# Two-layer branch decoder on one core: a reordered opening, squares summed on VectorE, and forty modulation tiles multiplied in pairs of high and low parts

## The chip, the cores and the metric

The kernel runs on one core of one Trainium2 chip. The metric is the device time of one execution in microseconds; the figure for a kernel is the median of its runs.

## What is computed

Two layers act on 520 token vectors of 1024 channels (512 prompt positions, 8 sample positions). There are nine conditioning vectors: one for the prompt, one for each sample. Cut to what matters:

```python
def trunk_layer(x, c, ...):
    mod = (jax.nn.silu(c) @ ada_w + ada_b)[:, None, :]            # 1024 -> 6 * 1024
    shift1, scale1, gate1, shift2, scale2, gate2 = jnp.split(mod, 6, axis=-1)
    h = rmsnorm(x, norm_g[0]) * (1.0 + scale1) + shift1
    z = h @ w_in
    ...                                 # three branches with gates, merged
    x = x + gate1 * (merged @ w_out)
    h2 = rmsnorm(x, norm_g[1]) * (1.0 + scale2) + shift2
    x = x + gate2 * peer(h2, peer_w_query, peer_sub_keys, peer_u, peer_v)
```

`rmsnorm` needs, for each token, the sum over 1024 channels of x². A final `rmsnorm` follows the second layer. All arithmetic is float32.

## The kernel before

**Layout.** A matrix is cut into tiles of 128 output channels by 1024 inputs (512 KB); channels lie on partitions in KC = 8 chunks of 128. A float32 tile is split into a high part, rounded to fp32r by ScalarE (`split` of `act`, L612, or `split_m`, L886), and a low part, the rest, by VectorE (`split` of `dve`, L993). TensorE multiplies high by high, high by low and low by high in `both` (L1515, L1516, L1518). One *product* is a tile times all tokens: 8 chunks, two halves of 260 tokens, 48 matmuls. Weights stand in a ring of four slots (`raw`, `w_hi`, `w_lo`); SyncE loads a tile once the one four before is split.

**Order.** Each engine's program is written out by hand, and semaphores join them. A layer's products are steps: `T_V` (0 to 3, gMLP v, done as tokens by channels in `v_parts`, L1610 to L1612), `T_U` (4), `T_B` (8), `T_C` (16), `T_BB` (24 to 27), `T_BR` (28 to 63: three branches b of 12 steps), `T_O` (64 to 71), then the query steps, 128 blocks up and 128 blocks down (L1827 to L1829).

**Modulation.** `ada_w` of a layer is 48 tiles. They are multiplied in plain float32, with the 9 columns of `cond_silu` stationary and the tile streaming. The first 16 (shift1 and scale1 of layer 1) go in four batches of four in `first_ada` (L1551). The other 80 are slipped in one by one behind products (`ada_tile`, L1567), by a table that gives each tile a step: `OWN_STEPS` for this layer's, `NEXT_STEPS` for the next layer's. Tiles come over ScalarE's DMA queue into the two slots of `ada_raw` (`load_ada`, L654). A batch of four tiles leaves a 9 x 512 row; ScalarE copies it out (`ada_rows`, L646), TensorE turns it by four transposes (`ada_turn`, L1576) and VectorE adds the bias (`take_ada`, L1047).

**Norms.** ScalarE squares a chunk of x (`square`, L631) into one of two buffers; TensorE sums over partitions with a stationary matrix of ones (`square_sum`, L1542), two float32 matmuls for each chunk; ScalarE takes the root (`std`, L637), VectorE inverts it (`root`, L1010), and `norm` and `modulate` form the new high and low parts (L1020, L679, L1025). There are five norms: two in each layer, and the final one, of which only the sums matter here. In this text norm 1 is layer 1's first, norm 2 its second, and so on to norm 5.

**Opening.** SyncE loads the conditions, the first batch, the biases (`ada_par`), the second batch, x, and batches three and four. GpSimd loads `par` and the convolution histories at once, ScalarE the first two `ada_raw` tiles. TensorE does batch, turn, batch, turn, four sums, batch, turn, four sums, batch, turn, and waits for `norm`.

**End of a layer.** The last down block releases the eight chunks of x one after another (L1494); ScalarE first splits one more tile, then loads the root's table and squares.

In the steps `T_BB` and `T_BR` VectorE also works off the 31-tap convolution, one instruction for each tap (L1179, `conv_c`), by the tables `BB_TAPS` and `BR_TAPS`.

## Time and profile before

| | us |
|---|---|
| runs (3): median, lowest, highest | 4106.55, 4103.54, 4110.15 |
| the profiled execution: its time | 4103.9 |
| its span, first to last instruction | 4102.1 |
| TensorE matmul busy | 4008.8 (98%) |
| VectorE busy | 2732.5 (67%) |
| ScalarE busy | 1584.2 (39%) |
| GpSimd busy | 812.4 (20%) |
| mean granted TensorE clock | 0.995 |

The profile is one execution recorded by the hardware. A row of a timeline gives start and duration in us, engine, line, operation, output and input tiles, a count of merged instructions and, in brackets, how long the engine had been idle and what ended that. Matmul durations overlap, since matmuls are pipelined: the spacing of starts is what one costs. A float32 matmul stands in the records twice, an fp32r matmul once.

### The profile page before, as it was taken

Reading aid. Unit: us, or ns where it says so; the run is one execution under the profiler, and the core shown is the slowest. Engines: PE = TensorE matmul, PEld = TensorE weight load, DVE = VectorE, ACT = ScalarE, POOL = GpSimd, SP = SyncE. Lnnn points to the kernel's source line nnn. Section 1 sums busy time; section 2 is a strip of 40 time slices with the busy share of each in tenths; the row PEclk is TensorE's granted clock in tenths of the full one; section 3 lists DMA queues with packets and bytes.
Section 4 is the critical chain, followed back from the end, with each engine's and each line's share of the span. In section 5 each row is a group of like instructions: output and inputs, shape, how many; then the busy total and the mean of one; then the engine's idle time right before and its main releaser. Section 6 shows DMA issues by size and latency. Waiting matters only on the chain.

```text
span 4102.1 us, 77256 instructions
## 1 busy us (share of the span) xinstructions
PE 4008.8 (98%) x29632; PEld 3893.8 (95%) x29632; DVE 2732.5 (67%) x4453; ACT 1584.2 (39%) x2673; POOL 812.4 (20%) x685
## 2 busy tenths in 40 slices
PE   6999999999999999999999999999999999999998
PEld 3899999999999999999989999899999999999998
DVE  2367638977666636777753775698776664477776
ACT  2222323333577733333332223333337775333332
POOL 1000000000122206555300000000002221356551
PEclk9999999999999999999999999999999999999999
DMA  4444332354466668999934532225445667799995
GB/s 171 140 113 134 103 117 77 118 166 136 128 190 193 192 202 315 345 352 352 336 128 114 134 109 83 78 89 170 136 137 160 187 190 208 238 352 345 352 349 185
DMA packets 418219, 781.87 MB, mean 191 GB/s; under 512 B 151184, under 2 KB 274448, under 8 KB 417344
## 3 DMA queue, kind: packets, MB, share of 16 engines
q1 hardware_dynamic: 176640, 441.70, 33.4%
q10 hardware_dynamic: 194240, 196.10, 15.2%
q0 software_dynamic: 47104, 141.00, 9.5%
q8 instruction: 140, 2.29, 0.3%
q14 instruction: 95, 0.78, 0.1%
HBM read 655.79 MB, written 122.88 MB: 190 GB/s over the span
## 4 chain that ended last, share of the span: by engine, by line
PE 95%; DVE 3%; ACT 1%; DMA 1%; issue 1%; DVEq 0%; SPq 0%; ACTq 0%; POOLq 0%
PE pg L1515 20%; PE pg L1518 19%; PE pg L1516 19%; PE pm L1827 5%; PE pg L1829 4%; PE pg L1828 4%; PE pm L1829 4%; PE pm L1828 4%; PE pg L1827 4%; PE pm L1567 3%; PE pm L1779 2%; DVE ys L1179 1%; PE pm L1542 1%; PE pm L1743 1%; DMA merged<-stream 1%; PE pm L1551 1%
## 5 line engine op out<-in xcount | busy, mean ns | idle before, releaser
L1515 PE MATMUL pg<-a_hi,w_hi 128*128 128x260 f32 x6400 | 1684.6, 284 | 25.1 <-DVE a_lo L1025 14.4
L1516 PE MATMUL pg<-a_lo,w_hi 128*128 128x260 f32 x6400 | 1667.2, 282 | 0.0
L993 DVE TENSOR_TENSOR w_lo<-raw,w_hi 128x1024 fp32r<-128x1024 f32 x688 | 841.2, 1225 | 1003.8 <-ACT w_hi L886 703.0
L1518 PE MATMUL pg<-a_hi,w_lo 128*128 128x260 f32 x6400 | 1290.0, 283 | 0.5 <-issue 0.5
L1515 PEld LDWEIGHTS pg<-a_hi,w_hi 128*128 128x128 f32 x6400 | 1208.7, 189 | 41.1 <-issue 37.1
L1516 PEld LDWEIGHTS pg<-a_lo,w_hi 128*128 128x128 f32 x6400 | 1205.6, 188 | 0.3
L1518 PEld LDWEIGHTS pg<-a_hi,w_lo 128*128 128x128 f32 x6400 | 987.1, 189 | 0.3 <-issue 0.2
L886 ACT CAST w_hi<-raw 128x1024 fp32r<-128x1024 f32 x500 | 525.7, 1051 | 784.9 <-PE pg L1829 739.6
L570 POOL DMA_INDIRECT rows<-stream,at_v x256 | 282.1, 1102 | 766.0 <-DVE acc_tok L1442 317.7
L580 POOL TENSOR_TENSOR one_j<-one_j,g_lo 128x896 fp32r<-128x896 f32 x112 | 189.3, 1690 | 1034.9 <-ACTq L914 1034.9
L618 ACT ACTIVATE hid<-pg 128x260 f32<-128x260 f32 x512 | 170.7, 386 | 517.0 <-PE pg L1518 497.1
L574 POOL DMA_INDIRECT hid_pick<-hid_tok,at_e x256 | 302.5, 1182 | 255.1 <-DMA hid_tok<-hid 177.7
L1442 DVE SCALAR_TENSOR_TENSOR acc_tok<-rows,coef,acc_tok 128x1024 f32<-128x1024 f32 x254 | 327.1, 1288 | 26.9 <-DVE hid_in L1425 12.0
L612 ACT CAST w_hi<-raw 128x1024 fp32r<-128x1024 f32 x188 | 196.2, 1048 | 323.8 <-PE pg L1518 298.4
L911 ACT ACTIVATE one_j<-one_j,g_hi 128x128 fp32r<-128x128 f32 x784 | 242.1, 390 | 163.1 <-DVEq L1409 163.1
L1179 DVE SCALAR_TENSOR_TENSOR ys<-glu,par,ys 128x512 f32<-128x512 f32 x240 | 180.3, 751 | 8.8
L1827 PE MATMUL pm<-h_hi,w_hi 128*128 128x392 f32 x512 | 177.4, 347 | 2.1 <-issue 2.1
L1827 PE MATMUL pm<-a_hi,w_hi 128*128 128x392 f32 x512 | 178.1, 348 | 0.0
L1829 PE MATMUL pg<-h_hi,w_lo 128*128 128x392 f32 x512 | 175.0, 342 | 0.0
L1829 PE MATMUL pm<-h_hi,w_lo 128*128 128x392 f32 x512 | 174.8, 341 | 0.0
L1827 PE MATMUL pg<-a_hi,w_hi 128*128 128x392 f32 x512 | 174.8, 341 | 0.0
L1828 PE MATMUL pg<-h_lo,w_hi 128*128 128x392 f32 x512 | 174.7, 341 | 0.0
(234 smaller groups left out, 5598.3 us busy)
## 6 DMA issues: line engine op xcount, KB each, us to landing
raw<-stream SPq DMA_DIRECT2D x688, 512.0 KB, 4.1
hidden_dram<-hid SPq DMA_DIRECT2D x256, 196.0 KB, 3.5
gate_dram<-gate_buf ACTq DMA_DIRECT2D x28, 1792.0 KB, 11.0
hid_in<-hidden_dram ACTq DMA_DIRECT2D x64, 784.0 KB, 6.1
gate_in<-gate_dram ACTq DMA_DIRECT2D x64, 784.0 KB, 11.0
ada_raw<-stream ACTq DMA_DIRECT2D x76, 512.0 KB, 3.4
hid_tok<-hid SPq DMA_DIRECT2D x256, 64.0 KB, 3.6
rows<-stream,at_v POOLq DMA_INDIRECT x256, 7.3
```

Source lines behind the costliest of these rows:

```text
L570: pool.indirect_dma_start(rows[:, k % ROWS, :], None, rows_v, bass.IndirectOffsetOnAxis(ap=at_v[:, k:k + 1], axis=0)).then_inc(row_in[k % ...
L574: pool.indirect_dma_start(hid_pick[:, k:k + 1], None, hid_elems, bass.IndirectOffsetOnAxis(ap=at_e[:, k:k + 1], axis=0)).then_inc(elem_in[ ...
L886: act.copy(ring(True, m % 4), raw[:, m % 4]).then_inc(hi_ready, 1)
L911: own.do(act.activation(one_j[:, n % 2, 0, t, :], one_j[:, n % 2, 1, t, :].bitcast(F32), ACT.Copy, scale=g_hi[:, n * GS + t:n * GS + t + 1 ...
L993: tt(ring(False, s), raw[:, s], ring(True, s).bitcast(F32), ALU.subtract).then_inc(lo_ready, 1)
L1442: dve.scalar_tensor_tensor(out=acc_tok[:, :], in0=v, scalar=coef[:, k:k + 1], in1=acc_tok[:, :], op0=ALU.mult, op1=ALU.add).then_inc(row_u ...
L1515: pe.matmul(outs[h], w[0], a[h][0], start=first, stop=False)
L1516: pe.matmul(outs[h], w[0], a[h][1], start=False, stop=False)
L1518: mm = pe.matmul(outs[h], w[1], a[h][0], start=False, stop=last)
L1827: pe.matmul(out, w_hi[:, j, d, :], hi[:, j, :], start=first, stop=False)
L1828: pe.matmul(out, w_hi[:, j, d, :], lo[:, j, :], start=False, stop=False)
L1829: mm = pe.matmul(out, w_lo[:, j, d, :], hi[:, j, :], start=False, stop=last)
```

## The change

1. **Opening.** The batches go in the order 2, 3, 0, 1 (scale first). x is loaded second; GpSimd's loads wait for the last batch, ScalarE's `ada_raw` loads come after `std`. TensorE does one batch, the eight sums, then the other three back to back with the turns in their middles, each batch in a PSUM bank of its own. The last turn moves behind chunk 0 of `v_parts`. `norm` scales chunks before the shifts are there.
2. **Pairs.** Forty of the 80 tiles are multiplied two at a time. ScalarE makes their high parts (`pair_hi`), VectorE the low ones (`pair_lo`), in buffers that overlay `merged` (early) or `ys` (late). The stationary operand is `c_parts`: 9 high and 9 low columns of the conditions. A pair is 16 fp32r matmuls of 256 columns (`ada_pair`). The row is then 18 x 512, and the turn is four float32 matmuls with `both_parts` (two stacked identities), which also add high and low rows. Pairs stand at steps 3, 5, 7, 9, 11, 13, 25, 27 (layer 2: from 7) and, for the next layer, at 53, 55, 57, 59, 61, 63. The 40 other tiles stay single.
3. **Sums of squares.** VectorE adds squares of chunks (`add_square`), so that TensorE sums fewer: 2 in place of 8 in norms 2 and 4, 6 in place of 8 in norms 3 and 5. Squares no longer wait for TensorE (their buffers reach into `merged`).
4. **Layer end.** ScalarE's last `split` goes behind the squares.
5. In layer 1 the two loads for step 5 are issued between ScalarE's splits of step 4's tiles.

```diff
-OWN_STEPS = (3, 3, 4, 5, *range(6, 14), *range(T_BB, T_BR), *range(T_BR, T_BR + 16))
+FIRST_ORDER = (2, 3, 0, 1)
+PAIR_EARLY, PAIR_LATE = (3, 5, 7, 9, 11, 13, T_BB + 1, T_BB + 3), tuple(range(T_BR + 25, T_O, 2))
+OWN_STEPS = (*(w for w in PAIR_EARLY for _ in range(2)), *range(T_BR, T_BR + 16))
 GAP_1, GAP_2 = T_V + 1, T_O + KC
-NEXT_STEPS = (*range(T_BR + 24, T_O + 2), GAP_2, GAP_2)
+NEXT_STEPS = (*(w for w in PAIR_LATE for _ in range(2)), T_O, T_O + 1, GAP_2, GAP_2)
...
+def sq_groups(j):
+    if j == 0:
+        return [[n] for n in range(KC)]
+    return [[*range(KC - 1)], [KC - 1]] if j % 2 else [[0], [1], [2], [3, 4], [5, 6], [7]]
...
-        ada_row = sb(ctx, "ada_row", [NC, 512])
+        ada_row = sb(ctx, "ada_row", [2 * NC, 512])
+        both_parts = sb(ctx, "both_parts", [2 * NC, NC])
+        c_parts = sb(ctx, "c_parts", [P, KC, 2 * NC], F32R)
...
+        early_hi = sb(early_pair, "early_hi", [P, 2, KC, P], F32R)
+        early_lo = sb(early_pair, "early_lo", [P, 2, KC, P], F32R)
...
+            if b < FIRST_BATCHES:
+                return pg[:, b // 2, b % 2]
...
-            for b in range(FIRST_BATCHES):
-                sp.dma_start(first_tiles[b], stream[4 * b:4 * b + 4].rearrange("n p k m -> p n k m")).then_inc(first_in[b], 16)
+            for b, n in enumerate(FIRST_ORDER):
+                sp.dma_start(first_tiles[b], stream[4 * n:4 * n + 4].rearrange("n p k m -> p n k m")).then_inc(first_in[b], 16)
                 if b == 0:
+                    sp.dma_start(x[:, :, :], x_t).then_inc(x_in, 16)
                     sp.dma_start(ada_par[:, :, :], ada_params).then_inc(ada_par_in, 16)
-                if b == 1:
-                    sp.dma_start(x[:, :, :], x_t).then_inc(x_in, 16)
...
+            own.link(pool.tensor_tensor(both_parts[:, :], ident[0:2 * NC, 0:NC], ident[0:2 * NC, NC:2 * NC], ALU.add))
...
+                    pool.wait_ge(first_in[FIRST_BATCHES - 1], 16)
...
-                if n >= 2:
-                    act.wait_ge(sq_used, l * (2 * KC) + (base * KC + n - 1))
+                if l + base == 0 and n >= 2:
+                    act.wait_ge(sq_used, n - 1)
...
-                act.activation(sq[:, n % 2, :], x[:, k, :], ACT.Square).then_inc(sq_ready, 1)
+                act.activation(square_of(l * 2 + base, n), x[:, k, :], ACT.Square).then_inc(sq_ready, 1)
...
+            def pair_hi(l, w):
+                g = pair_at(l, w)
+                if g is None:
+                    return
+                act.wait_ge(ada_used, g)
+                if w == PAIR_EARLY[0] or (l and w == PAIR_EARLY[2]):
+                    act.wait_ge(a_part, l * (2 * KC) + KC)
+                if w == PAIR_LATE[0]:
+                    act.wait_ge(y_ready, l * 3 + 2)
+                for z in range(2):
+                    n = RAW_TILES.index(g + z)
+                    act.wait_ge(ada_in[n % 2], (n // 2 + 1) * 16)
+                    act.copy(pair_parts(w)[0][:, z], ada_raw[:, n % 2]).then_inc(pair_hi_ready, 1)
...
+                if l == 0 and w == 0:
+                    act.wait_ge(mod_taken, FIRST_BATCHES)
+                    for k in range(4):
+                        prompt(k, k + 1)
+                    ada_rows(3)
+                    act.wait_ge(mod_taken, FIRST_BATCHES + 1)
+                    for k in range(4, KC):
+                        if k == 6:
+                            of_samples(KC + 1)
+                        prompt(k, k + 1)
+                    return
...
+                    act.wait_ge(x_in, 16)
+                    square(l, 0, 0)
+                    square(l, 0, 1)
+                    ada_rows(0)
+                    for n in range(2, KC):
+                        square(l, 0, n)
+                    std(l, 0, 1.0 / D)
                     for g in loads_first(0):
                         load_ada(g)
-                    ada_rows(0)
                     ada_rows(1)
-                    act.wait_ge(x_in, 16)
-                    for n in range(4):
-                        square(l, 0, n)
+                    for k in range(4):
+                        split(l, 0, k)
                     ada_rows(2)
-                    for n in range(4, KC):
-                        square(l, 0, n)
-                    split(l, 0, 0)
-                    split(l, 0, 1)
-                    ada_rows(3)
-                    split(l, 0, 2)
-                    split(l, 0, 3)
...
+                    act.wait_ge(prod, (l - 1) * NM + (M_ED + NBLK))
+                    split(l, 0, 3)
+                    std(l, 0, 1.0 / D)
...
+                freed = loads_at(l, T_U)
                 for k in range(4):
                     split(l, 1, k)
+                    if freed and k % 2:
+                        act.wait_ge(ada_used, before(freed[k // 2]) + 1)
+                        load_ada(freed[k // 2])
...
-                for block in range(NBLK - 4 if l == DEPTH - 1 else NBLK):
+                for block in range(NBLK - 4 if l == DEPTH - 1 else NBLK - 1):
...
+                        scaled(k)
+                        if k:
+                            split(l, k - 1, k - 1)
+                    take_ada(2)
+                    scaled(4)
+                    low(0, 1)
+                    split(l, 3, 3)
+                    for k in range(1, 4):
+                        low(k, k + 1)
+                        scaled(k + 4)
+                    scaled_samples()
+                    take_ada(3)
+                    shifted_samples()
+                    low(4, 5)
+                    low(5, 6)
+                    low_samples(7)
+                    low(6, 8)
+                    low(7, 9)
...
+            def add_square(l, base, n):
+                dve.wait_ge(sq_ready, l * (2 * KC) + (base * KC + n + 1))
+                group = next(g for g in sq_groups(l * 2 + base) if n in g)
+                sum_ = square_of(l * 2 + base, group[0])
+                own.link(tt(sum_, sum_, square_of(l * 2 + base, n), ALU.add))
+                if n == group[-1]:
+                    dve.sem_inc(sq_added, 1)
...
+            def pair_lo(l, w):
+                g = pair_at(l, w)
+                if g is None:
+                    return
+                hi, lo = pair_parts(w)
+                for z in range(2):
+                    dve.wait_ge(pair_hi_ready, 2 * pairs_before(g) + z + 1)
+                    tt(lo[:, z], ada_raw[:, RAW_TILES.index(g + z) % 2], hi[:, z].bitcast(F32), ALU.subtract).then_inc(pair_lo_ready, 1)
...
+                    take_ada(0)
+                    dve.wait_ge(x_in, 16)
+                    root(0)
+                    take_ada(1)
                     scale_of(l, 0)
-                    dve.wait_ge(x_in, 16)
-                split(l, 2, 2)
-                split(l, 3, 3)
...
+                    if k >= 2:
+                        add_square(l, 1, k - 1)
...
+                for n in (4, 6):
+                    add_square(l + 1, 0, n)
...
-                if b >= 2:
-                    pe.wait_ge(mod_taken, b)
                 for k in range(KC):
+                    if b >= 2 and k == KC // 2:
+                        ada_turn(b - 1)
...
+            def ada_pair(g):
+                b, h = g // 4, g % 4 // 2
+                if h == 0:
+                    pe.wait_ge(mod_taken, b)
+                pe.wait_ge(pair_lo_ready, 2 * pairs_before(g) + 2)
+                out = ada_bank(b)[0:2 * NC, 2 * h * P:2 * (h + 1) * P].rearrange("p (s m) -> p s m", s=2)
+                for k in range(KC):
+                    for z, part in enumerate(pair_parts(TILE_STEP[g][1])):
+                        mm = pe.matmul(out, c_parts[:, k, :], part[:, :, k, :], start=k + z == 0, stop=k + z == KC)
+                mm.then_inc(ada_used, 2)
...
+                    if paired(4 * b):
+                        mm = pe.matmul(to, ada_row[:, s * P:(s + 1) * P], both_parts[:, :], start=True, stop=True)
+                    else:
+                        mm = pe.transpose(to, ada_row[0:NC, s * P:(s + 1) * P], ident[0:NC, 0:NC])
...
+                    first_ada(0)
+                    for n in range(KC):
+                        square_sum(l, 0, n)
+                        if n == 3:
+                            ada_turn(0)
+                    first_ada(1)
+                    first_ada(2)
+                    first_ada(3)
...
+                    if l == 0 and k == 0:
+                        ada_turn(3)
...
-                    if k >= 2:
-                        square_sum(l, 1, k - 2)
-                square_sum(l, 1, KC - 2)
+                square_sum(l, 1, 0)
                 gap = tiles_at(l, GAP_2)
                 for g in gap[0:1]:
                     ada_tile(g)
-                square_sum(l, 1, KC - 1)
+                square_sum(l, 1, 1)
```

TensorE at the opening (`first_ada` L1551, turn L1576, sums L1542), before:

```order
L1551 MATMUL pm<-raw,cond_silu 9x512 x8
L1576 MATMUL pm<-ident,ada_row 128x9 x4
L1551 MATMUL pm<-merged,cond_silu 9x512 x8
L1576 MATMUL pm<-ident,ada_row 128x9 x4
L1542 MATMUL pm<-sq,ones 128x260 x8
L1551 MATMUL pm<-ys,cond_silu 9x512 x8
L1576 MATMUL pm<-ident,ada_row 128x9 x4
L1542 MATMUL pm<-sq,ones 128x260 x8
L1551 MATMUL pm<-last_first,cond_silu 9x512 x8
L1576 MATMUL pm<-ident,ada_row 128x9 x4
L1610 MATMUL pm<-w_hi,a_hi 128x512
```

The same place now (L1723, L1764, L1714; `v_parts` from L1804):

```order
L1723 MATMUL pg<-raw,cond_silu 9x512 x8
L1714 MATMUL pm<-sq,ones 128x260 x8
L1764 MATMUL pg<-ident,ada_row 128x9 x4
L1714 MATMUL pm<-sq,ones 128x260 x8
L1723 MATMUL pg<-merged,cond_silu 9x512 x8
L1723 MATMUL pg<-ys,cond_silu 9x512 x4
L1764 MATMUL pg<-ident,ada_row 128x9 x4
L1723 MATMUL pg<-ys,cond_silu 9x512 x4
L1723 MATMUL pg<-last_first,cond_silu 9x512 x4
L1764 MATMUL pg<-ident,ada_row 128x9 x4
L1723 MATMUL pg<-last_first,cond_silu 9x512 x4
L1804 MATMUL pm<-w_hi,a_hi 128x512
```

All eight sums now stand ahead of three of the four batches, and one turn has left this stretch.

VectorE in steps 26 and 27 of layer 1 (L1193: take a product; L993: low part of a weight tile; L1179: taps), before:

```order
L1193 TENSOR_TENSOR ys<-pg,ys 128x260 x2
L993 TENSOR_TENSOR w_lo<-raw,w_hi 128x1024
L1179 SCALAR_TENSOR_TENSOR ys<-glu,par,ys 128x512 x6
L1193 TENSOR_TENSOR ys<-pg,ys 128x260 x2
L993 TENSOR_TENSOR w_lo<-raw,w_hi 128x1024
L1179 SCALAR_TENSOR_TENSOR ys<-glu,par,ys 128x512 x6
```

Now (L1352, L1094 and L1338 are the same three; L1191 is `pair_lo`):

```order
L1352 TENSOR_TENSOR ys<-pg,ys 128x260 x2
L1191 TENSOR_TENSOR early_lo<-ada_raw,early_hi 128x1024 x2
L1094 TENSOR_TENSOR w_lo<-raw,w_hi 128x1024
L1338 SCALAR_TENSOR_TENSOR ys<-glu,par,ys 128x512 x6
L1352 TENSOR_TENSOR ys<-pg,ys 128x260 x2
L1094 TENSOR_TENSOR w_lo<-raw,w_hi 128x1024
L1338 SCALAR_TENSOR_TENSOR ys<-glu,par,ys 128x512 x6
```

Two low parts of modulation tiles stand ahead of the split and the taps.

## Rows read from the trace of the kernel before

**Rows 1.** Page, part 1: busy us (share of the span), instructions

```profile
PE 4008.8 (98%) x29632; PEld 3893.8 (95%) x29632; DVE 2732.5 (67%) x4453; ACT 1584.2 (39%) x2673; POOL 812.4 (20%) x685
```

**Rows 2.** Timeline of TensorE, opening: start us, us, instruction, [idle before, releaser]

```profile
16.65 8.62 PE L1551 MATMUL pm<-raw,cond_silu 128*9 128x512 f32 x16 [16.65 <-DMA raw<-stream]
26.91 7.04 PE L1551 MATMUL pm<-merged,cond_silu 128*9 128x512 f32 x16 [0.45 <-DMA merged<-stream]
35.36 3.89 PE L1542 MATMUL pm<-sq,ones 128*128 128x260 f32 x16 [0.24 <-ACT sq L631]
59.30 0.38 PE L1576 MATMUL pm<-ident,ada_row 9*128 9x9 f32 x4 [0.80 <-ACTq L647]
70.52 0.77 PE L1610 MATMUL pm<-w_hi,a_hi 128*128 128x512 f32 x1 [10.84 <-DVE a_lo L1025]
```

**Rows 3.** SyncE's issues (start us), then DMA issues of the opening (KB, us to landing)

```profile
3.30 0.43 SPq L456 DMA_DIRECT2D merged<-stream  x1
5.24 13.22 SPq L456 DMA_DIRECT2D last_first<-stream  x1
...
merged<-stream SPq DMA_DIRECT2D x1, 2048.0 KB, 23.6
last_first<-stream SPq DMA_DIRECT2D x1, 2048.0 KB, 36.9
```

**Rows 4.** Stretches: us, busy us of each engine, PEclk, DMA share, GB/s

```profile
60.00:74.00 14.00, 3.48 (x8) 2.81 (x9) 13.48 (x20) 7.40 (x12) 0.00 (x0) 0.53 0.24 76
115.00:119.00 4.00, 4.00 (x23) 3.08 (x21) 0.00 (x0) 0.00 (x0) 0.00 (x0) 0.57 0.48 166
```

**Rows 5.** Timeline of TensorE: step 4 of layer 1, and of layer 2

```profile
114.51 2.72 PE L1567 MATMUL pm<-ada_raw,cond_silu 128*9 128x128 f32 x16 [4.27 <-DMA ada_raw<-stream]
...
2137.98 0.39 PE L1515 MATMUL pg<-a_hi,w_hi 128*128 128x260 f32 x1 [3.18 <-DVE w_lo L993]
```

**Rows 6.** Timeline of ScalarE, each row once a product has ended: steps with a tile, then without

```profile
266.90 1.04 ACT L612 CAST w_hi<-raw 128x1024 fp32r<-128x1024 f32 x1 [6.73 <-PE pg L1518]
274.68 1.04 ACT L612 CAST w_hi<-raw 128x1024 fp32r<-128x1024 f32 x1 [6.74 <-PE pg L1518]
...
429.61 0.67 ACT L618 ACTIVATE sig<-pg 128x260 f32<-128x260 f32 x2 [5.29 <-PE pg L1518]
...
435.37 0.67 ACT L618 ACTIVATE sig<-pg 128x260 f32<-128x260 f32 x2 [3.86 <-PE pg L1518]
```

**Rows 7.** Timeline of TensorE: seven fp32r matmuls of 256 columns, and what follows

```profile
1342.77 1.00 PE L1779 MATMUL pm<-one_j,one_i 128*128 128x256 f32 x7
1343.60 0.28 PE L1515 MATMUL pg<-a_hi,w_hi 128*128 128x260 f32 x1
```

**Rows 8.** Page, part 5: two groups, busy us, mean ns, idle before

```profile
L993 DVE TENSOR_TENSOR w_lo<-raw,w_hi 128x1024 fp32r<-128x1024 f32 x688 | 841.2, 1225 | 1003.8 <-ACT w_hi L886 703.0
...
L1179 DVE SCALAR_TENSOR_TENSOR ys<-glu,par,ys 128x512 f32<-128x512 f32 x240 | 180.3, 751 | 8.8
```

**Rows 9.** Timelines of VectorE (two `T_O` steps) and TensorE (norm 2), layer 1

```profile
603.93 0.17 DVE L1277 TENSOR_TENSOR tmp<-pg,mod 128x8 f32<-128x8 f32 x1 [3.98 <-PE pg L1518]
...
610.56 0.17 DVE L1277 TENSOR_TENSOR tmp<-pg,mod 128x8 f32<-128x8 f32 x1 [3.98 <-PE pg L1518]
...
616.99 1.92 PE L1542 MATMUL pm<-sq,ones 128*128 128x260 f32 x8
```

**Rows 10.** Timelines of TensorE (norms 3 and 5) and VectorE (last four x chunks)

```profile
2090.09 7.60 PE L1542 MATMUL pm<-sq,ones 128*128 128x260 f32 x32 [3.16 <-ACT sq L631]
...
4082.07 7.53 PE L1542 MATMUL pm<-sq,ones 128*128 128x260 f32 x32
...
4081.42 2.71 DVE L1494 SCALAR_TENSOR_TENSOR x<-pg,mod,x 128x512 f32<-128x512 f32 x4
```

**Rows 11.** `ada_raw` loads: all 76 (least, median, most us to landing); one issued in 255 to 264 us

```profile
DMA to landing us min/median/max: 3.1/3.4/14.6
...
ada_raw<-stream ACTq DMA_DIRECT2D x1, 512.0 KB, 13.1
```

More of the change, by code:

```diff
@@ L91, in tiles_at, with paired, pair_at, pairs_before @@
     return [g for g in TILE_STEP if TILE_STEP[g] == (l, w)]
+def paired(g):
+    return TILE_STEP.get(g, (0, 0))[1] in PAIR_EARLY + PAIR_LATE
+def pair_at(l, w):
+    return next((g for g in tiles_at(l, w) if paired(g)), None)
+def pairs_before(g):
+    return sum(paired(i) for i in TILE_STEP if i < g) // 2
 def before(g):
```

131 lines of the change are left out of this document (91 added, 40 removed).

## Prediction

> **What bounds the kernel now.** I read the page's busy times first: TensorE's matmuls fill 98% of the span [rows 1]. So a step that TensorE sheds is time gained, unless another engine then makes it wait. The timeline of TensorE shows the waits: one cluster is in the opening, where matmuls begin at 16.65 and the products (`v_parts`) only at 70.52, after 10.84 us of waiting for norm 1 [rows 2]. Its clock was 0.53 from 60 to 74 us and 0.57 from 115 to 119 us, so part of both stretches ran at 1.2 GHz in place of 2.4; each follows an idle spell [rows 2, 4, 5]. Elsewhere the cost of a piece is read from the spacing of steps.
>
> **The sum, part by part.** All figures are from the profiled execution.
>
> *A. Opening.* SyncE's queue lands in order. The second batch landed at 3.30 + 23.6 = 26.9, the last at 5.24 + 36.9 = 42.1, with three 2 MB transfers (x, batch three, batch four) in between and after: 5.1 us each [rows 3]. The first came at 16.65, while GpSimd's and ScalarE's loads ran beside it [rows 2]. Those now start later, so for the first batch I take an issue at 3.3 at the latest, 5.1, and 0.8 for the ramp, 9.2 (bounds: 16.65 if nothing improves, 8.4 without a ramp), 14.3 for x, 19.6, 24.7 and 29.8 for the rest. From there TensorE is the chain, with its data always ahead: first batch 8.6, eight sums 2 x 3.89 = 7.8, three batches at 7.04 and three turns at about 0.5 with their gaps [rows 2]: 9.2 + 8.6 + 7.8 + 21.1 + 1.5 = 48.2. ScalarE's row copies, four splits, and VectorE's scaled chunks fit beside the last two batches if the four weight tiles land by about 42 (alone they would at 34.9). `v_parts` starts at about 48.3 in place of 70.5: 22.2. TensorE arrives there without an idle spell, so the slow start goes: from 70.52 it ran at half clock to 74 and a little beyond, 4 us, worth 2.0. The fourth turn now stands inside `v_parts`: -0.5. **A = 23.7.** What is late next: shift chunks 4 to 7 (`take_ada(3)`) are wanted 11 us after the start and ready in about 5.
>
> *B. Pairs.* A step with a tile takes 274.68 - 266.90 = 7.78, one without 435.37 - 429.61 = 5.76 [rows 6]: a tile costs 2.02, two 4.04. A pair is 16 fp32r matmuls of 256 columns; no row has such a pair, the nearest are seven of 256 columns in 1343.60 - 1342.77 = 0.83, or 0.119 each [rows 7]: 1.90. It could be as dear as two tiles (4.04); below 1.90 I see no reason in the rows. 20 pairs x 2.14 = 42.8. The Trainium skill (TensorE: Matmul & The Clock Gate, section Back-to-back issue gap) gives 81 ns a matmul at 128 columns and 131 ns at 512 in a stream with weight loads; interpolated that is an estimate of about 98 ns at 256 columns, a pair at 1.57 and 6.6 us more gain; rows 7 speak against it.
>
> Ten batches now turn by float32 matmuls. Four transposes took 0.38 [rows 2]; four float32 matmuls are eight records. Between no more than now and eight at a single tile's 0.12 (+0.6) I take +0.35: -3.5. At step 3 of layer 1 two tiles covered a wait for the first split of step 4: layer 2, with no tile there, waited 3.18 [rows 5]. A pair covers 1.9: -1.3.
>
> VectorE and ScalarE get 40 more passes each; VectorE's is 1.22 [rows 8]. Steps 24 to 27 are the tight place: four takes (about 0.8), four splits, 22 taps at 0.75 and four low parts make 3.2 + 4.9 + 16.5 + 4.9 = 29.5 for VectorE [rows 8], against 4 x 5.76 + 2 x 1.90 = 26.8 for TensorE (31.1 before). The backlog of 2.7 is hidden, since weights are split up to three steps ahead, and from step 28 on single tiles are back (7.78 a step against 7 taps and a split, 6.5). The pair at step 27 has another problem: its loads are issued only after the pair at 25, in a stretch where a load took 13.1 to land [rows 11]. A pair is due two products, 11.5, after its loads; the second cast (1.04 [rows 6]) after the first, and the second low part, take 3.3; so it waits once landing exceeds 8.2. At 13.1 that is 4.9; at the median 3.4 it is 0. I take 1.5 for layer 1 and none for layer 2. **B = 42.8 - 3.5 - 1.3 - 1.5 = 36.5.**
>
> *C. Step 4 of layer 1.* TensorE waited 4.27 there for a tile, and then ran at a clock of 0.57 over 4 us, that is at half for 3.4 of them, 1.7 lost [rows 4, 5]. Step 4 has no tile now, and step 5's loads are issued some us earlier. **C = 6.0**, between 4.3 and 6.0.
>
> *D. Norms 2 and 4.* The steps of `T_O` are 610.56 - 603.93 = 6.63 apart [rows 9]; less 5.76 a sum costs 0.88 (0.93 back to back [rows 9]). Six fall away in norm 2: 5.3. In norm 4 the sixth was followed by a wait for the last square anyway, so I count five: 4.4. VectorE's adds (520 columns, some 0.65 by the 1.22 of 1024 [rows 8]) lie in its idle 3.98 of each step [rows 9]. **D = 9.7.**
>
> *E. Norm 3.* TensorE idled 3.16 for the first square and summed for 7.60 [rows 10]. The idle came from ScalarE, which split a tile and loaded a table first; with the split behind, squares follow x. Two sums fewer are 1.9. **E = 5.0**; the chain to norm and products behind it moves as one. Bound below: 1.9, if squares are still late.
>
> *F. Norm 5.* No idle there [rows 10], so two of eight sums: **F = 1.9**. VectorE finishes x at 4084.1 and two adds at 4085.5; the last sum but one would be wanted at 4085.8.
>
> Sum: 23.7 + 36.5 + 6.0 + 9.7 + 5.0 + 1.9 = 82.8. Against the profiled 4103.9 that gives 4021.1. The median of the runs is 2.65 above that execution, so for a median I say 4023.8.
>
> **Rivals.**
> 1. *The opening's weights are late.* GpSimd's and ScalarE's 2.7 MB now compete with the four weight tiles. Before, the same traffic moved the second batch from about 14.3 to 26.9, 12.6 us [rows 3]. Put on the tiles' 34.9 it gives 47.5; then split 1.0, row copy and turn 1.1 and half a batch 3.5: start at 53.2, 4.9 later, 4029. For it: the same bytes. Against: fewer wide transfers are in flight. The Trainium skill (DMA: Bandwidth & Descriptors, section Issuing engines are not separate DMA queues) says that transfers of all engines end on the same 16 engines and interleave, which is this rival's way; at equal shares that page would have the tiles done near 40, in time (an estimate).
> 2. *Pairs run faster* than rows 7, by the page's spacing named above: 4023.8 - 6.6 = 4017.
> 3. *Pairs save nothing*: with 18 stationary columns, or by waits, a pair costs its 4.04. B's 36.5 goes: 4060. Against it: rows 7.
> 4. *Slower than before: modulation loads bind.* 15 of the 20 pairs have their loads issued only after the pair before them. Each us of landing above 8.2 costs TensorE 15 us. At 13.7 on average the whole gain is gone; at 14.6, the longest seen [rows 11], it is 15 x 6.4 = 96, and 4120. Against it: the median is 3.4.
>
> **How the numbers follow.** Forecast 0.79, rival 1 0.12, rival 2 0.04, rival 3 0.04, rival 4 0.01. Low end: turns free (3.5), no wait at 27 (1.5), pairs by rival 2 (6.6) and a bit of run scatter: 4010. High end: rival 1 (+4.9), waits of 4.9 at step 27 in both layers (+8.3), turns at their upper bound (+2.5), scatter of 3: 4042. Rivals 3 and 4 are left out. A measurement of this kernel tells about 0.2% (8 us) from no change. Every case but the fourth is faster by more: faster 0.98, same 0.01, slower 0.01.
>
> **What would show it.** `v_parts` starting at 47 to 53 us with the clock full; 16 pair matmuls within 1.9; a turn of a paired batch within 0.6 to 1; steps with a pair 13.4 for two; no idle at step 4; 6.6-us `T_O` steps at 5.8; sums of norm 3 starting with no gap. Wrong would be: idle of TensorE in front of pairs, named by VectorE's low parts; a lower clock in the trunk; or TensorE behind VectorE's taps after step 24.

## The result, and the profile after

The changed kernel takes 4056.58 us (median of 4 runs, 4055.82 to 4058.12) against 4106.21 for the kernel before beside it: a ratio of 0.9879, 95% interval 0.9862 to 0.9896. That is 49.6 us saved where 82.8 were forecast; the predicted 4024 us and its range of 4010 to 4042 lie below. The profiled spans are 4102.1 and 4054.6, a gain of 47.5 us. Some of the runs below stood beside slower executions of the kernel before (4124.04 and 4130.88 us), so those are judged by their ratio to it and by a gain that leaves the experts out.

The page's busy line is in [rows 1]. The same line now:

```profile
PE 3969.7 (98%) x29288; PEld 3871.9 (95%) x29288; DVE 2789.2 (69%) x4510; ACT 1621.4 (40%) x2714; POOL 818.9 (20%) x686
```

TensorE's busy time fell by 39.1 us; the rest of the gain is waiting. TensorE's timeline of the opening [rows 2], step 4 of each layer [rows 5], and the last sum of norms 2 and 4 and the first of norm 5 [rows 9, 10]:

```profile
10.41 8.75 PE L1723 MATMUL pg<-raw,cond_silu 128*9 128x512 f32 x16 [10.41 <-DMA raw<-stream]
22.91 0.41 PE L1764 MATMUL pg<-ident,ada_row 9*128 9x9 f32 x4
80.77 0.39 PE L1681 MATMUL pg<-a_hi,w_hi 128*128 128x260 f32 x1 [1.34 <-DVE w_lo L1094]
...
2089.41 0.58 PE L1681 MATMUL pg<-a_hi,w_hi 128*128 128x260 f32 x1 [3.19 <-DVE w_lo L1094]
...
575.50 1.14 PE L1714 MATMUL pm<-merged,ones 128*128 128x260 f32 x4
2568.25 1.15 PE L1714 MATMUL pm<-merged,ones 128*128 128x260 f32 x4 [1.22 <-ACT merged L688]
4036.65 1.92 PE L1714 MATMUL pm<-sq,ones 128*128 128x260 f32 x8
```

The first batch is there at 10.41 in place of 16.65, `v_parts` begins at 48.66 in place of 70.52, and the stall of 4.27 us at step 4 of layer 1 is gone. The new trouble shows in TensorE's timeline of steps 25 to 29, where [rows 6] had a steady 7.78 a step. Both layers:

```profile
225.98 0.28 PE L1752 MATMUL pm<-early_hi,c_parts 128*18 128x256 f32 x1
240.75 0.29 PE L1752 MATMUL pm<-early_hi,c_parts 128*18 128x256 f32 x1 [1.25 <-DVE early_lo L1191]
248.45 1.05 PE L1762 MATMUL pm<-both_parts,ada_row 18*128 18x9 f32 x8
256.60 3.39 PE L1739 MATMUL pm<-ada_raw,cond_silu 128*9 128x128 f32 x16 [7.09 <-DMA ada_raw<-stream]
...
2250.81 0.40 PE L1752 MATMUL pm<-early_hi,c_parts 128*18 128x256 f32 x1 [3.46 <-DVE early_lo L1191]
2266.80 3.52 PE L1739 MATMUL pm<-ada_raw,cond_silu 128*9 128x128 f32 x16 [4.69 <-DMA ada_raw<-stream]
```

The pair of step 27 waits, and the single tile of step 28 waits longer. One stretch of layer 1 and two of layer 2 (columns as in [rows 4]) give the clock there: near 0.5 over some 7 us each, the lower of its levels 1.2 and 2.4 GHz, from within the wait on; the tile of step 28 takes 3.39 and 3.52 us in place of 1.92.

```profile
253.00:260.00 7.00, 3.40 (x17) 2.12 (x17) 3.88 (x6) 1.71 (x3) 0.00 (x0) 0.52 0.59 218
...
2249.00:2256.00 7.00, 5.19 (x25) 4.21 (x26) 6.29 (x8) 2.98 (x4) 0.00 (x0) 0.55 0.20 75
2263.00:2270.00 7.00, 3.20 (x16) 2.02 (x16) 3.87 (x6) 1.71 (x3) 0.00 (x0) 0.52 0.58 211
```

What issues the late load is in ScalarE's timeline, and whom ScalarE waited for:

```profile
228.11 0.82 ACTq L714 DMA_DIRECT2D ada_raw<-stream  x2
236.40 1.05 ACT L729 CAST early_hi<-ada_raw 128x1024 fp32r<-128x1024 f32 x1 [9.16 <-DMA ada_raw<-stream]
238.39 1.05 ACT L729 CAST early_hi<-ada_raw 128x1024 fp32r<-128x1024 f32 x1 [0.94 <-DMA ada_raw<-stream]
...
253.35 0.82 ACTq L714 DMA_DIRECT2D ada_raw<-stream  x2
254.22 0.67 ACT L675 ACTIVATE sig<-pg 128x260 f32<-128x260 f32 x2 [10.83 <-DVEq L1357]
```

The two loads for the pair of step 27 leave at 228.11 and are 8 to 10 us on the way. The loads for steps 28 and 29 could leave once the pair is multiplied, at 242.6, but leave at 253.35: ahead of branch one ScalarE's program waits for `src_ready`, which VectorE gives (L1357) when the taps of step 27 are done. Its timeline: 248.52 + 4.68 = 253.20.

```profile
248.52 4.68 DVE L1338 SCALAR_TENSOR_TENSOR ys<-glu,par,ys 128x512 f32<-128x512 f32 x6
```

Where the 47.5 us come from: the same instruction of TensorE is taken in both traces, and its start of before less its start now is the gain so far. Beside it stands the forecast for the same stretch, from the prediction's own terms.

```
stretch, up to the start of               gain so far   of it here   forecast
the tile or pair of step 3, layer 1          23.2          23.2        23.7
the transposes of v_tok, layer 1             38.1          14.8        16.5
the tile or pair of step 25                  40.8           2.8         2.0
the tile of step 29                          32.4          -8.4         0.4
the convolution's sums (step 49)             32.2          -0.2         0
the tile of step 64                          39.9           7.7        11.8
the queries (norm 2)                         45.2           5.3         5.3
v of layer 2 (experts, norm 3)               48.6           3.4         5.0
the transposes of v_tok, layer 2             54.4           5.8         7.9
the pair of step 25                          55.9           1.5         2.0
the tile of step 29                          45.0         -10.9         1.9
the sums of squares of step 50               42.9          -2.1         0
the queries (norm 4)                         46.9           4.0         4.4
the sums of norm 5 (experts)                 45.4          -1.5         0
the end                                      47.5           2.1         1.9
```

Two short stretches, steps 25 to 29 of each layer, hold 21.6 of the 35.3 us that are missing. The -2.1 of layer 2 is mostly clock: the convolution's sums took 5.46 us at 2426.86 where they took 3.78 before. The experts lost time in both layers: 2.3 us in layer 1, where the gain was 45.2 at the queries and 42.9 at the last products (the row of `acc_tok` at 2083.45 before, at 2040.55 now), and 1.5 in layer 2. These losses stay unexplained; the run of part 5 shows none.

### The profile page after: what moved, and what is told of

It reads as the page before. It is cut to its first block, busy times and chain, and to the rows that moved or that the text cites. A ratio compares the mean times of both kernels' runs of the same rounds, so it can differ in the third digit from the quotient of the medians.

```text
span 4054.6 us, 76683 instructions
## 1 busy us (share of the span) xinstructions
PE 3969.7 (98%) x29288; PEld 3871.9 (95%) x29288; DVE 2789.2 (69%) x4510; ACT 1621.4 (40%) x2714; POOL 818.9 (20%) x686
## 4 chain that ended last, share of the span: by engine, by line
PE 94%; DVE 4%; DMA 1%; ACT 1%; issue 1%; DVEq 0%; ACTq 0%; SPq 0%; POOLq 0%
PE pg L1681 19%; PE pg L1684 19%; PE pg L1682 19%; PE pm L2021 5%; PE pg L2021 5%; PE pg L2022 5%; PE pm L2022 5%; PE pg L2023 4%; PE pm L2023 4%; PE pm L1973 2%; PE pm L1739 2%; DVE ys L1338 1%; PE pm L1752 1%; PE pg L1723 1%; DMA ada_raw<-stream 1%; PE pm L1937 1%
## 5 line engine op out<-in xcount | busy, mean ns | idle before, releaser
L1094 DVE TENSOR_TENSOR w_lo<-raw,w_hi 128x1024 fp32r<-128x1024 f32 x688 | 841.2, 1224 | 910.0 <-ACT w_hi L987 597.2
L1338 DVE SCALAR_TENSOR_TENSOR ys<-glu,par,ys 128x512 f32<-128x512 f32 x240 | 180.3, 751 | 8.9
L2021 PE MATMUL pg<-h_hi,w_hi 128*128 128x392 f32 x512 | 175.1, 342 | 0.0
L2022 PE MATMUL pm<-a_lo,w_hi 128*128 128x392 f32 x512 | 174.6, 341 | 0.0
```

Of the source, the lines that this page charges most:

```text
L1094: tt(ring(False, s), raw[:, s], ring(True, s).bitcast(F32), ALU.subtract).then_inc(lo_ready, 1)
L2021: pe.matmul(out, w_hi[:, j, d, :], hi[:, j, :], start=first, stop=False)
L2022: pe.matmul(out, w_hi[:, j, d, :], lo[:, j, :], start=False, stop=False)
```

## The experiments

Each run is read on two scales beside its time. The **distance** is from the pair (or tile) of step 25 to the tile of step 29, layer 1 / layer 2: before the change 31.46 / 31.46, in the changed kernel 39.88 / 42.35. The **trunk gain** leaves the experts out: the gain so far at layer 1's queries, and what is added to it between v and the queries of layer 2. For the changed kernel it is 45.2 - 1.7 = 43.5. A second profile of it (part 7) gives 39.2, and distances of 42.57 / 44.70: the same kernel differs by 4.3 us in the one and by 2.4 to 2.7 in the other, and every run has one profile. The experts are left out because in some runs TensorE waits there for VectorE's gating, which the change does not touch (3.74 us in the changed kernel's second profile, 8.13 and 5.12 in the best version of part 7).

**1. Late issue.** ScalarE's loads for steps 28 and 29 are put ahead of its wait.

```
+                ada_before(l, T_BR)
                 act.wait_ge(early_out, (l + 1) * (16 * (2 + BC)))
                 act.wait_ge(src_ready, l * 3 + 2)
```

> The changed kernel, with ScalarE's issue of the two loads for steps 28 and 29 put ahead of its wait for VectorE's convolution taps. Theory (the loads are issued late): they leave at about 243.5 us in layer 1 in place of 253.35 and land by 250; TensorE's 7.09 and 4.69 us waits at the tile of step 28 go, and with them the half clock that follows (1.4 and 1.6): 14.8 us in all, span 4039.8 against 4054.6. From the pair of step 25 to the tile of step 29: 31.4 us in layer 1, about 36 in layer 2. Rival 1 (landing is slow there, whenever the loads leave): they still take 10 us, the waits shrink by 4 at most, span 4050. Rival 2 (ScalarE and VectorE themselves are behind): the tile's wait goes but comes back in front of product 30 or 31, named by the sigmoid or a low part; span over 4050.

Measured: 4045.34 us, ratio 0.985 (0.9833 to 0.9866), span 4041.9; the distance 35.05 / 36.08. TensorE has no wait at the tile of step 28 in either layer. The run is 12.7 us shorter by its span, near the 14.8 expected. Layer 1 came out 3.7 short, because the pair of step 27 waited longer, with half clock behind it:

```profile
243.17 0.40 PE L1754 MATMUL pm<-early_hi,c_parts 128*18 128x256 f32 x1 [3.54 <-DVE early_lo L1193]
2247.45 0.40 PE L1754 MATMUL pm<-early_hi,c_parts 128*18 128x256 f32 x1 [4.88 <-DVE early_lo L1193]
```

**2. Loads freed by the low parts.** In addition, the loads behind the pairs of steps 25 and 27 wait for VectorE's low parts, after which `ada_raw` is free, and not for TensorE.

```
+                for g in loads_at(l, w):
+                    act.wait_ge(pair_lo_ready, 2 * pairs_before(before(g)) + before(g) % 2 + 1)
+                    load_ada(g)
```

> As the run before, and the loads behind the pairs of steps 25 and 27 are also issued once VectorE has made the low parts, not once TensorE has multiplied the pair. Theory: the pair of step 27 gets its data 4 us earlier, its waits of 1.25 (layer 1) and 3.46 us (layer 2) go, and the half clock in layer 2 with them (2.6): 7 us more than the run before, span 4033, and 30 us from the pair of step 25 to the tile of step 29 in both layers. Rival (ScalarE's or VectorE's order holds the low parts, not the landing): span within 2 us of the run before.

Measured: 4039.22 us, ratio 0.9832 (0.9816 to 0.9848), span 4040.8, distance 34.10 / 33.95. The loads left 5 us earlier, at 223.15, and the pair still waited 2.78 and 2.65 us: a miss for the theory, and the rival's bound in the span (within 2 us), but not for its reason. The span is that of the slowest of four executions, though, beside the fastest of part 1; by the medians this run is 6.1 us lower, near the theory's 7, and which of the waits were shorter in the other three executions no profile shows. In ScalarE's timeline the cast waits for a load that is 15.7 us on the way:

```profile
223.15 1.74 ACTq L714 DMA_DIRECT2D ada_raw<-stream  x2
238.82 1.05 ACT L729 CAST early_hi<-ada_raw 128x1024 fp32r<-128x1024 f32 x1 [11.28 <-DMA ada_raw<-stream]
```

So the landing itself is slow here. What runs beside it is in GpSimd's timeline of the changed kernel, the stores of the convolution history:

```profile
218.60 0.72 POOL L613 DMA_DIRECT2D hc_p<-glu  x1 [49.28 <-DVEq L1325]
219.25 3.60 POOL L615 DMA_DIRECT2D hc_s<-glu_s  x4
```

**3. The same, with these stores held back** until step 30.

```
                 pool.wait_ge(glu_ready, l + 1)
+                pool.wait_ge(y_ready, l * 3 + 1)
                 pool.dma_start(hc_p...
```

> The second run's kernel (loads behind the low parts), with GpSimd's stores of the convolution history (hc_p, hc_s) held back until step 30. In that run the loads of the pair of step 27 left at 227.0 us of layer 2's stretch (2227.0) and landed only 10 to 14 us later, beside those stores. Theory (the stores hold the transfer engines): without them the loads land in 3 to 5 us, the pair of step 27 waits for nothing (2.78 and 2.65 us before), and the half clock behind it goes: span 4040.8 - 5.4 - 2.6 = 4033. Rival (SyncE's weight stream, or the loads' own size, makes them slow): they still take 9 us and more, the span stays within 2 us of 4040.8.

Measured: distance 29.84 / 29.84, the full clock over all of it, and no wait of TensorE between 215 and 262 us. The two transfer tables for the 20 us behind step 25 (first the changed kernel's, then this one's; queue, packets, MB, share of the 16 engines; last column us to landing) show the cause:

```profile
q1 hardware_dynamic: 432, 1.57, 35.3%
q0 software_dynamic: 76, 0.16, 20.7%
...
ada_raw<-stream ACTq DMA_DIRECT2D x2, 512.0 KB, 9.0
```

```profile
q1 hardware_dynamic: 432, 1.57, 22.7%
...
ada_raw<-stream ACTq DMA_DIRECT2D x2, 512.0 KB, 3.9
```

The stores' queue (q0) moves 0.16 MB in that time and takes 20.7% of the transfer engines; without it the same 432 packets of SyncE's queue (q1) take 22.7% in place of 35.3%, and the loads land in 3.9 us in place of 9.0. That is what the Trainium skill (DMA: Bandwidth & Descriptors, section Issuing engines are not separate DMA queues) says of transfers from different engines: they end on the same 16 and interleave. The trace agrees.

The time of this run: 4051.42 us, ratio 0.982 (0.9802 to 0.9837), trunk gain 66.3 against the changed kernel's 43.5 (39.2 in its second profile).

**4. The stores alone.** This run has the change of part 3 and nothing of parts 1 and 2.

> The changed kernel with nothing but the history stores held back until step 30; ScalarE's order of loads is as in the changed kernel. Theory (there are two causes, slow landing beside the stores and late issue behind VectorE's taps): the pair of step 27 waits for nothing any more in either layer (1.25 and 3.46 us before), its loads landing in about 4 us; but the loads of the tile of step 28 still leave only when the taps are done, at about 251 us, so TensorE still waits 5 to 7 us there in both layers, at half clock behind it: 37 to 39 us from the pair of step 25 to the tile of step 29 (39.9 and 42.4 now). Rival 1 (slow landing is the whole cause): 30 to 32 us there in both layers. Rival 2 (late issue is the whole cause): 39 us and more in both.

Measured: 4050.18 us, ratio 0.9863 (0.9846 to 0.9879), span 4048.1, distance 37.23 / 37.29, as the theory of two causes had it. The pair of step 27 waits for nothing; ScalarE issues at 251.43, again behind the taps, and TensorE waits at step 28:

```profile
254.61 3.58 PE L1740 MATMUL pm<-ada_raw,cond_silu 128*9 128x128 f32 x16 [5.66 <-DMA ada_raw<-stream]
2261.63 3.59 PE L1740 MATMUL pm<-ada_raw,cond_silu 128*9 128x128 f32 x16 [5.72 <-DMA ada_raw<-stream]
```

**5. No pairs at steps 25 and 27.** `PAIR_EARLY` loses its last two entries, and steps 24 to 27 get a single tile each.

> The changed kernel, with the two pairs of steps 25 and 27 put back to four single tiles at steps 24 to 27. Theory (the pairs there only lost, because a pair's loads leave late): steps 25 to 29 take 31.5 us in both layers as before the change (39.9 and 42.4 now), 19.3 us less, and the tile of step 24 costs 2.0 a layer: span 4039.3. Rival (the opening and the earlier pairs brought TensorE nearer to VectorE's taps, so that the stretch waits whatever the tiles' form): waits of 4 us and more stay there, span over 4047.

Measured: 4039.87 us, ratio 0.9834 (0.9818 to 0.9851), span 4038.0 against 4039.3 expected. From the tile of step 25 to that of step 29: 31.84 / 35.16 (one wait of 2.04 us in layer 2). Fewer pairs are faster here by 16.6 us (15.3 expected), though each pair by itself saves 2.2. Only part of this is the theory's: the trunk gain rises by 12.8 (56.3 against 43.5), and the remaining 3.8 are the experts' losses that this run does not have. Once the loads come in time, the pairs pay after all: the kernel of part 3, with pairs at steps 25 and 27, has a trunk gain of 66.3.

**6. The turns.** Four transposes of 18 rows in place of four float32 multiplications by `both_parts`; VectorE adds the halves.

```
-                        mm = pe.matmul(to, ada_row[:, s * P:(s + 1) * P], both_parts[:, :], start=True, stop=True)
+                    mm = pe.transpose(ada_bank(b)[:, s * rows:(s + 1) * rows], ada_row[0:rows, s * P:(s + 1) * P], ident[0:rows, 0:rows])
...
+                if rows > NC:
+                    own.link(tt(to, to, turned[:, :, NC:2 * NC], ALU.add))
```

> The changed kernel, with the turn of a paired batch as four transposes of 18 rows, and VectorE adding the two halves from PSUM. Theory (a float32 multiplication is what makes the turn dear): each of ten turns takes 0.35 to 0.45 us in place of 1.18, 7 to 8 us in all, span 4047. Rival 1 (18 rows cost twice what 9 cost): 0.7 to 0.8 a turn, 4 us, span 4050.5. Rival 2 (what a turn saves is lost at the next wait, since the slack behind it is short): under 2 us, span over 4052.5.

Measured: 4056.31 us, ratio 0.9873 (0.9857 to 0.989), span 4056.4: nothing gained. Yet the turn itself did shrink (the changed kernel's row, then this run's):

```profile
127.97 1.05 PE L1762 MATMUL pm<-both_parts,ada_row 18*128 18x9 f32 x8
```

```profile
250.73 0.42 PE L1765 MATMUL pm<-ident,ada_row 18*128 18x18 f32 x4
257.35 3.58 PE L1743 MATMUL pm<-ada_raw,cond_silu 128*9 128x128 f32 x16 [6.21 <-DMA ada_raw<-stream]
```

At the transposes of `v_tok` in layer 1 TensorE was 0.9 us ahead of the changed kernel, at the convolution's sums 2.3 behind (distance 42.21 / 43.80). I read this as: what it saved, it waited. It is not shown, since the changed kernel's second profile has distances as long. The Trainium skill (Perfetto Trace Analysis, section Transposes) asks that a transposition be done as one and not as a matmul; the rows agree, 0.42 against 1.05. With what stands in front and behind, two steps with a pair and a turn take 13.90 us here (120.40 to 134.30) where the changed kernel takes 14.53, and 13.36 without a turn: a turn costs 0.54 in place of 1.17. So each saves 0.63 us; the 0.76 of the next expectations set the row's 0.42 against a cost in all. The turns were tried again on the kernel of part 5:

> Singles at steps 24 to 27 (span 4038.0 in the run before) with the turns by transposes. The turns by transposes alone brought nothing (4056.4 against 4054.6) though each took 0.42 us in place of 1.18. Theory (what they saved ahead of step 28 was lost again at the late loads there, whose end VectorE sets): with that wait away the eight turns left save 0.76 each, 6 us, span 4032. Rival (VectorE's extra addition or the longer rows cost as much elsewhere, so that transposes never pay): span 4038 within 1.5.

Measured: 4047.83 us, ratio 0.9818 (0.978 to 0.9856), trunk gain 58.9 against 56.3 for the run of part 5: 2.6 us for eight turns, between theory (6, or 5.0 at 0.63 a turn) and rival (0). The three late turns of layer 1 gave 1.8 of it, 0.6 each, by the gain between the convolution's sums and the queries (14.8 against 13.0). The three early ones brought `v_tok`'s transposes 1.7 forward, although the wait in front of those grew from 1.6 to 1.8 us; by the convolution's sums 1.1 of it was lost, which is one wait of TensorE that the run of part 5 does not have:

```profile
186.28 0.28 PE L1688 MATMUL pg<-a_hi,w_lo 128*128 128x260 f32 x1 [1.13 <-issue]
```

The profile names no releaser for it, and the cause was not tried.

**7. All together, and one more.** Loads behind the low parts, stores held back, turns by transposes; beside it the changed kernel again, and a version with the copies of y ahead of the pair's casts.

> The changed kernel once more, as the base for the two beside it. Both theories: 4054.6 span as in its first profile where the expert stage is undisturbed; in any case 29 to 31 us of gain left behind step 30 of layer 1 and a gap of 37 to 44 us from the pair of step 25 to the tile of step 29 in each layer.

> The changed kernel with three edits: loads behind the low parts, history stores held back, turns by transposes. Theory (the causes are separate and add up): against the changed kernel the loads and stores give 17 to 18 us, as the kernel with held-back stores showed up to the expert stage (62.4 of gain against 46.3 at the same product), and ten turns 7.6 (now that nothing behind them waits): 25 us under the run beside it. Rival (TensorE then reaches VectorE's taps or the copies of y sooner, and waits there): 18 us or less, with new waits between steps 28 and 60.

> As e10, and in every third step of a branch the copies of y (y_hi, y_lo) stand ahead of the pair's casts and low parts. Theory (the 1.62 us wait of the changed kernel in front of the first y product of branch three is the pair's casts and low parts standing ahead of the copies of y): that wait goes, 1.5 to 2.5 us under e10. Rival (it only changes places: the pair of step 55 or the tile of weights behind is late by as much): within 0.5 us of e10.

```
                     median us   ratio to before (95%)      distance
changed, again        4074.74    0.9879 (0.9857 to 0.9902)  42.57 / 44.70
all three             4045.13    0.9794 (0.9771 to 0.9817)  29.18 / 29.18
and y first           4060.88    0.9838 (0.9817 to 0.9859)  29.18 / 29.18
```

The second is the best version: 29.6 us under the changed kernel beside it and 85.8 under before, trunk gain 69.8 against 39.2. The theory's 25 is exceeded, with other parts: loads and stores gave 27.1 (part 3's 66.3 against 39.2) for 17 to 18, and the turns 3.5 on top of that, not 7.6. Beside the stores, now behind step 30, the tile of step 33 waits 1.07 us. Putting y first only changed places, as its rival said: the wait in front of y went, and the pair of step 55 waited 2.10. The run is 15.8 us slower than the one without it where the rival allowed 0.5, but that is not the order of y. In the trunk it lacks 9.6 us, and all of that stands from step 29 to step 35 (54.17 and 51.07 us in the two layers against 48.26 and 47.12), where the tile of step 33 waited 4.29 and 2.22 us beside the same stores, with half clock behind it. By what more the medians differ no profile shows:

```profile
290.55 3.58 PE L1754 MATMUL pm<-ada_raw,cond_silu 128*9 128x128 f32 x16 [4.29 <-DMA ada_raw<-stream]
459.77 0.29 PE L1767 MATMUL pm<-late_hi,c_parts 128*18 128x256 f32 x1 [2.10 <-DVE late_lo L1202]
```

Holding the stores back beyond the single tiles, to step 44 or so, was not tried.

**8. Two parts of the sum, undone.** First the sums of squares go back to TensorE, eight to a norm; the order of the squares stays.

> The changed kernel with all sums of squares behind the opening back on TensorE, eight to a norm, as before the change; the order of the squares stays. Theory (a sum costs TensorE 0.88 to 0.93 us wherever it stands): norm 2 +5.3, norm 4 +3.1 to 4.4, norms 3 and 5 +1.9 each, 12.2 to 13.5 us, span 4067. Rival (in the norms the last square's chain sets the end, and TensorE's sums run in its shadow): norms 3, 4 and 5 give under 1 us each, span 4060 to 4062.

Measured: 4098.92 us, ratio 0.9926 (0.9899 to 0.9953). By the trace the sums are worth 5.3 us in norm 2 (gain from the convolution's sums to the queries 7.6 against 12.9), 1.5 in norm 3 and 1.5 in norm 5 (TensorE's sums take 7.2 in place of 5.7), 4.1 in norm 4: 12.4, inside the theory's 12.2 to 13.5. The median is some 24 above the changed kernel's of part 7 (19 by the two ratios); the rest is mostly a 10.1 us wait in the experts. Then GpSimd's wait in the opening is taken away.

> The changed kernel without GpSimd's wait for the last opening batch, so that its loads of the layer's small tables run beside the opening's batches again. Theory (they compete for the transfer engines): the first batch lands at 13 to 15 us in place of 10.4, the next ones 3 to 8 late, v_parts starts at 52 to 56 us in place of 48.7, span 4058 to 4062. Rival (the new order on SyncE's queue alone made the opening short): v_parts at 48.7 within 0.5, span 4054.6.

```profile
14.49 9.40 PE L1721 MATMUL pg<-raw,cond_silu 128*9 128x512 f32 x16 [14.49 <-DMA raw<-stream]
```

The first batch lands at 14.49 in place of 10.41 and `v_parts` starts at 53.38 in place of 48.66: 4.7 us of the opening's gain come from holding GpSimd's loads back, the rest, as I read it, from the order of the batches and the later start of ScalarE's loads, which were not tried apart. The total (4073.65, ratio 0.9876, 0.9855 to 0.9897) cannot be told from the changed kernel's in part 7 (0.9879).

## Why the prediction was wrong

**Right: the opening (A).** 23.2 us against 23.7. `v_parts` started at 48.66 for a forecast of 48.3, at the full clock, and rival 1 (late weights) did not come. Two small errors cancel in it: the first batch landed at 10.41 for 9.2 (no row shows the 0.8 that I took for a ramp), and TensorE's chain behind it took 38.3 for 39.0.

**Right: the pair by itself.** Layer 1's first steps without any wait:

```profile
106.91 0.28 PE L1752 MATMUL pm<-early_hi,c_parts 128*18 128x256 f32 x1
...
108.76 0.28 PE L1681 MATMUL pg<-a_hi,w_hi 128*128 128x260 f32 x1
...
120.27 0.28 PE L1752 MATMUL pm<-early_hi,c_parts 128*18 128x256 f32 x1
```

A pair takes 1.85 us (forecast 1.90), and two steps with one 13.36 (forecast 13.4), 2.20 less than the 15.56 of two steps with tiles. So rival 2 is refuted, and so is the price that rival 3 gave a pair. But rival 3 also said "or by waits", and its 4060 is nearer to the 4056.6 measured than my forecast: with C at its 6.0, the stretches that hold B add up to 5.0 us of its 36.5. The pairs gave almost nothing in all, mostly by waits around one pair in each layer and not by their own cost. The spacing here is 0.116 us a matmul, where rival 2 stood on an estimate of 0.098 from the Trainium skill (TensorE: Matmul & The Clock Gate, section Back-to-back issue gap): the measurement decides. The matmuls of 512 columns in `v_parts` differ from that page too: they start 0.23 apart (48.99, 49.22, 49.45) for its 0.131.

**Wrong, the main step: "the pair at step 27 has another problem", 1.5 us for layer 1 and none for layer 2.** I saw that a pair's loads leave late, put a price on the pair, and stopped there. The price was too small (1.25 and 3.46 us; 2.80 and 5.05 when run again): I took the median landing for layer 2, where the same history stores run beside the loads in every layer. The trace of before could have told me, by a load issued at 2283.98 beside its stores of 2281.00 to 2285.31 (KB, us to landing):

```profile
ada_raw<-stream ACTq DMA_DIRECT2D x1, 512.0 KB, 10.3
```

At 10.3 my own rule (what exceeds 8.2) gives 2.1 us of waiting for layer 2. And I did not ask who comes behind the pair. The single tiles of steps 28 and 29 share its two buffers, so their loads can leave only once the pair is multiplied, and they stood in ScalarE's program behind its wait for VectorE's taps. Before the change this wait cost nothing. ScalarE's timeline of before has the loads for steps 28 and 29:

```profile
276.60 0.33 ACTq L654 DMA_DIRECT2D ada_raw<-stream  x1
...
289.52 0.33 ACTq L654 DMA_DIRECT2D ada_raw<-stream  x1
```

The first left 13.9 us ahead of its tile (290.48), long before the wait. The second was held by the same wait for some 5 us, and still left 8.7 ahead of its tile (298.26), more than the median landing of 3.4 [rows 11]. Now TensorE waited 7.09 and 4.69 us for the tile of step 28, at half clock behind it. I had even worked out that VectorE needs 29.5 us for steps 24 to 27 against TensorE's 26.8, and called the 2.7 hidden because weights are split three steps ahead. For weights that is so; for the loads that ScalarE issues behind VectorE's taps it is not. Rival 4 (modulation loads bind) had the right mechanism at the wrong place: it priced 15 pairs alike, and it is one pair a layer and the tile behind it. Parts 1 to 4 show this: issuing in time gives 12.7 us by the span (11.7 by the trunk gain), faster landing alone 6.5 (5.1), and both, with the loads behind the low parts, 22.8 by the trunk gain, or 27.1 against the changed kernel's second profile. In the two stretches themselves the distances fell by 10.0 and 12.5, 22.5 in all. That is somewhat more than the 21.6 missing there, since the 1.5 that I had allowed at step 27 went too.

**Too small: the turn.** I took +0.35 between 0 and 0.6; from 13.36 and the 14.53 of a step pair with a turn (120.27 to 134.80) it is 1.17 in all, 0.83 more than the transposes' 0.34. Ten turns are 8.3, not 3.5. The spacing of my bound was right: the eight records at 100.07 end with the next product at 101.06, 0.12 apart as in a single tile. I had no row for taking about half of the bound, and I left out 0.2 us beside the records: 0.09 of gap in front, and 0.10 by which the product's second matmul follows its first later. A turn in front of a single tile shares this with the tile (131.64 to 131.98 before, 0.34 in all).

**Missed: the late pairs of layer 1.** Six pairs with their turns gave 7.7 us for a forecast of 11.8. Turns account for 1.4; two waits, in TensorE's timeline, for 2.5:

```profile
464.96 0.36 PE L1681 MATMUL pg<-y_hi,w_hi 128*128 128x260 f32 x1 [1.62 <-issue]
521.87 0.36 PE L1681 MATMUL pg<-a_hi,w_hi 128*128 128x260 f32 x1 [0.85 <-issue]
```

The first has no releaser in the profile, but VectorE's timeline does show one: its low part of y ends at 462.47 + 2.33 = 464.80, because two casts and two low parts of the pair stand ahead of the copies of y.

```profile
458.38 2.49 DVE L1191 TENSOR_TENSOR late_lo<-ada_raw,late_hi 128x1024 fp32r<-128x1024 f32 x2 [2.19 <-ACT late_hi L729]
460.79 1.22 DVE L1094 TENSOR_TENSOR w_lo<-raw,w_hi 128x1024 fp32r<-128x1024 f32 x1
462.47 2.33 DVE L1417 TENSOR_TENSOR y_lo<-ys,y_hi 128x2080 fp32r<-128x2080 f32 x1 [0.47 <-ACTq L915]
```

Part 7 shows that putting y first moves this wait and does not remove it. What the second waits for was not tried.

**C.** The stall of step 4 in layer 1 went, 6.0 as taken. In layer 2 the old wait (3.19) stayed, now with half clock behind it, which is most of what that stretch lacks (5.8 for 7.9); its two dearer turns are the rest. At the full clock, in the changed kernel's second profile, the transposes of `v_tok` gained 7.3 us from step 4 on, against 5.9.

**D, E, F.** Norm 2 gave its 5.3 exactly, norm 4 4.0 for 4.4 though its last sum waits 1.22 us for the last square. Norm 3 gave 5.7 for 5.0 (48.6 less the 42.9 at the experts' last products), which the experts' own -2.3 hides in the table; norm 5 1.8 by TensorE's own rows (the sums from 4036.65 end at 4042.35, 5.70 against 7.53), 1.9 forecast.

## What to carry to other kernels

When a step is made cheaper by joining two, the buffers it holds are freed two at a time and later: find the next user of each buffer, the instruction that issues its load, and everything that instruction stands behind on its engine's queue. A load's landing time is that of its own stretch: look which other queue's transfers run there before taking a median. And try the plain fix first: here moving one line got back 12.7 of the 35.3 us missing, and leaving two pairs out in each layer 16.6.

## What the runs showed of the hardware that I had not expected

- Small stores from GpSimd slow other transfers far beyond their bytes: in 20 us 0.16 MB took 20.7% of the transfer engines (part 3), and two 512 KB loads landed in 9.0 to 15.7 us beside them, 3.6 to 4.5 without.
- Four float32 multiplications of 18 rows by 9 columns cost TensorE 1.17 us in all, four transposes of the same 18 rows 0.54. By their rows it is 1.05 against 0.42, and four transposes of 9 rows have 0.41.
- Behind the same wait of 3.19 us at step 4 of layer 2 the clock differs from run to run. Over the 8 us from there, first in the changed kernel's two profiles, then in the run of part 6 with pairs:

```profile
2089.41:2097.41 8.00, 8.00 (x54) 8.00 (x55) 4.46 (x6) 4.80 (x7) 0.00 (x0) 0.80 0.73 264
```

```profile
2091.62:2099.62 8.00, 8.00 (x66) 8.00 (x67) 4.49 (x7) 6.04 (x8) 0.00 (x0) 1.00 0.77 260
```

```profile
2090.45:2098.45 8.00, 8.00 (x45) 8.00 (x46) 4.46 (x6) 4.31 (x5) 0.00 (x0) 0.65 0.74 263
```

Of the two levels, 1.2 and 2.4 GHz, the lower held for about 3.2 us, not at all, and for about 5.6: up to 2.8 us of the time for nothing that the kernel did differently at that place. A forecast of a few microseconds cannot do without that much of a margin.
